# Nine pairs of seven block products in the last network's input half, two weight sums in device memory, and another order of the last products

## The chip, the cores and the metric

The kernel runs on one core of one Trainium2 chip, in float32. The metric is the device time of one execution in microseconds (us), the median of several runs.

## What is computed

One layer of a diffusion backbone on 512 latent tokens and 256 context tokens of width 1024: a gated network (input 1024 to 2 x 2816, output 2816 to 1024), a token mixer, and a second gated network for the latent tokens alone. The change is in the second network:

```python
def swiglu(h, w_in, w_out):
    gate, up = jnp.split(h @ w_in, 2, axis=-1)
    return (jax.nn.silu(gate) * up) @ w_out

x = residual_post_norm(x, swiglu(modulate(x, m, 2), ffn2_w_in[l], ffn2_w_out[l]), m[:, 8], FFN_HALF, ln_gain[2], ln_bias[2])
```

Here h is 512 x 1024, w_in is 1024 x 5632 (the left half gives the gate, the right half "up") and w_out is 2816 x 1024.

## The kernel before, in words

**Precision.** Each float32 operand is split into a high part (rounded to the type fp32r) and a low part (the rest). `product` (L2197) issues three matmuls for one product: low by high (L2199), high by low (L2200), high by high (L2201). A weight tile comes by DMA into one of two raw buffers `w_raw` (8 KB per partition, 1 MB in all); ScalarE writes its high part (`split_hi`, L957), then VectorE its low part (`split_lo`, L1448). The split tiles have two slots each in most of the kernel, three in the last network.

**Order of the work.** All weights are loaded in the order of one list, `JOBS`. Every engine walks the same list by loops written out by hand: `load` on the queue of SyncE (SP), `split_hi` on ScalarE (ACT), `split_lo` on VectorE (DVE), the products on TensorE (PE). A raw buffer is loaded again once the low part of the job that used it is written; jobs i and i+2 share a raw buffer. The splits of job i+2 are issued while PE works on job i. Each engine runs its instructions in order.

**Stages**, in time of the profile: L1, the first network on the latent tokens, to about 413 us; C, the same network on the 256 context tokens (22 input jobs, then output jobs) to about 600; the mixer (six groups of heads, g = 0 to 5) to about 946; its output projection and the norms to about 1000; L2, the second network, to the end. An input job of C is 48 matmuls of 256 columns, one of L1 or L2 has 48 matmuls of 512 columns (2 blocks of 128 output columns, gate and up, x 8 tiles of the contraction x 3).

**L2's input half** has 22 such jobs (`last_ffn` on each engine: L1054 ACT, L1707 DVE, L2366 PE). Per job ACT applies silu to the gate's PSUM bank (L1066) and DVE multiplies it with the other bank into `hid_last` (L1717). **L2's output half** is already done as seven block products in place of eight (Winograd's form): `SEVEN` is their order, each in 3 steps by 2 token tiles; sums of blocks of `hid_last` are formed on DVE (L1649), sums of blocks of w_out in device memory. PSUM banks X, Y and Z collect the products; `keep` copies an early sum out (ACT L1052), `join` combines a late one with it (DVE L1675).

**GpSimd (POOL)** issues through its own DMA queue: blocks of w_ada in L1 (L826), and in the mixer `copy_weights` (L888) and `add_weights` (L891), DMAs from device memory to device memory that copy a block of w_out and add another to it.

## Time and profile before

| | |
|---|---|
| median of 3 runs | 1336.09 us (1335.64 to 1336.14) |
| the profiled execution | 1336.66 us, span 1334.8 us |
| TensorE busy | 1307.2 us, 98% of the span; granted clock 0.994 on average |
| VectorE busy | 825.3 us, 62% |
| ScalarE busy | 546.5 us, 41% |
| DMA | 206.74 MB, mean 155 GB/s |

The span runs from the first to the last instruction. The profiled execution took 1.86 us more than its span and 0.57 us more than the median. A matmul's recorded duration overlaps with its neighbours', so the pace of matmuls is read from their starts.

### The profile page before, as it was taken

What the parts mean: (1) busy time and instruction counts of PE and PEld (TensorE: products, weight loads), DVE (VectorE), ACT (ScalarE), POOL (GpSimd) and SP (SyncE); (2) the same over time, 40 slices, a digit from 0 to 9 for tenths busy, and PEclk for the clock granted to TensorE, in tenths of its full rate; (3) what the DMA queues carried; (4) which work ended last, traced back from release to release, by engine and by line L of the source; (5) the groups of instructions that cost most, each with busy time, mean ns of one, the idle gap of its engine ahead of it and who ended that gap; (6) DMA issues with size and microseconds to landing.
All of it is one profiled execution on the core that took longest, in us unless ns stands there. A gap on an engine that the chain in (4) does not pass through costs nothing.

```text
span 1334.8 us, 17708 instructions
## 1 busy us (share of the span) xinstructions
PE 1307.2 (98%) x7134; PEld 1102.9 (83%) x7134; DVE 825.3 (62%) x1165; ACT 546.5 (41%) x740; POOL 83.0 (6%) x91
## 2 busy tenths in 40 slices
PE   8999999999999999999999999999999999999996
PEld 5778888888889999888888888887788888888885
DVE  5446688666686777565227678878763223335888
ACT  5525221222212544565325645556552222224553
POOL 1000000000000000000202221220000000000000
PEclk8999999999999999999999999999999999999998
DMA  9965545665545667553432478266435333333562
GB/s 320 275 180 175 186 164 164 185 180 172 178 158 156 177 189 190 174 174 126 138 122 64 83 200 220 54 148 150 142 95 158 95 111 95 96 95 110 190 205 102
DMA packets 217378, 206.74 MB, mean 155 GB/s; under 512 B 7322, under 2 KB 175880, under 8 KB 216592
## 3 DMA queue, kind: packets, MB, share of 16 engines
q1 hardware_dynamic: 202328, 151.39, 38.5%
q0 software_dynamic: 14272, 52.53, 13.9%
q10 hardware_dynamic: 696, 1.68, 0.4%
q8 instruction: 57, 0.93, 0.3%
q14 instruction: 25, 0.20, 0.0%
HBM read 203.46 MB, written 25.18 MB: 171 GB/s over the span
## 4 chain that ended last, share of the span: by engine, by line
PE 84%; DVE 6%; ACT 3%; issue 2%; DMA 2%; SPq 2%; DVEq 0%; ACTq 0%
PE ps L2199 27%; PE ps L2201 26%; PE ps L2200 26%; DMA w_raw<-ffn_w_in 1%; DVE w_lo L1448 1%; DMA gain_bias_b<-w_ada 1%; PE ps L2238 1%; SPq L770 1%; PE ps L2662 1%; PE ps L2647 1%; ACT w_hi L957 1%; PE ps L2251 0%; PE ps L2681 0%; SPq L766 0%; DVE xl L1570 0%
## 5 line engine op out<-in xcount | busy, mean ns | idle before, releaser
L2199 PE MATMUL ps<-h_hi,w_lo 128*128 128x512 f32 (+1 forms) x1120 | 391.5, 350 | 1.9 <-DVE w_lo L1796 1.4
L2201 PE MATMUL ps<-h_hi,w_hi 128*128 128x512 f32 (+1 forms) x1120 | 387.7, 346 | 0.0
L2200 PE MATMUL ps<-h_lo,w_hi 128*128 128x512 f32 (+1 forms) x1120 | 387.7, 346 | 0.0
L1448 DVE TENSOR_TENSOR w_lo<-w_raw,w_hi 128x2048 fp32r<-128x2048 f32 (+1 forms) x116 | 256.3, 2210 | 157.9 <-ACT w_hi L957 157.7
L957 ACT ACTIVATE w_hi<-w_raw 128x2048 fp32r<-128x2048 f32 (+1 forms) x116 | 214.2, 1848 | 274.0 <-PE ps L2201 259.9
L2199 PEld LDWEIGHTS ps<-h_hi,w_lo 128*128 128x128 f32 x1120 | 211.7, 189 | 32.2 <-issue 4.2
L2201 PEld LDWEIGHTS ps<-h_hi,w_hi 128*128 128x128 f32 x1120 | 211.7, 189 | 27.0
L2200 PEld LDWEIGHTS ps<-h_lo,w_hi 128*128 128x128 f32 x1120 | 211.8, 189 | 25.5
L2199 PE MATMUL ps<-w_hi,h_lo 128*128 128x512 f32 x298 | 117.0, 393 | 1.4 <-DVE w_lo L1448 1.4
L1460 DVE SCALAR_TENSOR_TENSOR ada_row<-ada_block,c_cols,ada_row 128x256 f32<-128x256 f32 x224 | 108.6, 485 | 8.0
L2199 PE MATMUL ps<-h_hi,half_lo 128*128 128x512 f32 (+1 forms) x272 | 101.9, 375 | 0.7 <-ACT beside_lo L1286 0.4
L1717 DVE TENSOR_TENSOR hid_last<-ps,glu 128x512 f32<-128x512 f32 x22 | 15.2, 692 | 139.4 <-ACT glu L1066 139.4
L2201 PE MATMUL ps<-w_hi,h_hi 128*128 128x512 f32 x256 | 99.7, 389 | 0.0
L2200 PE MATMUL ps<-w_lo,h_hi 128*128 128x512 f32 x256 | 99.6, 389 | 0.0
L2201 PE MATMUL ps<-h_hi,half_hi 128*128 128x512 f32 (+1 forms) x272 | 97.6, 359 | 0.0
L2200 PE MATMUL ps<-h_lo,half_hi 128*128 128x512 f32 (+1 forms) x272 | 97.5, 358 | 0.0
L1066 ACT ACTIVATE glu<-ps 128x512 f32<-128x512 f32 x22 | 13.2, 598 | 172.8 <-PE ps L2201 172.8
L2199 PE MATMUL ps<-w_hi,hid_lo_lat 128*128 128x512 f32 x176 | 69.6, 396 | 0.0
L2201 PE MATMUL ps<-w_hi,hid_hi_lat 128*128 128x512 f32 x176 | 68.6, 390 | 0.0
L2200 PE MATMUL ps<-w_lo,hid_hi_lat 128*128 128x512 f32 x176 | 68.5, 389 | 0.0
L2199 PEld LDWEIGHTS ps<-w_hi,h_lo 128*128 128x128 f32 x298 | 56.0, 188 | 13.8 <-DVE w_lo L1448 2.3
L2199 PEld LDWEIGHTS ps<-h_hi,half_lo 128*128 128x128 f32 x272 | 51.3, 189 | 10.5 <-issue 2.8
(297 smaller groups left out, 1699.5 us busy)
## 6 DMA issues: line engine op xcount, KB each, us to landing
w_raw<-ffn_w_in SPq DMA_DIRECT2D x124, 512.0 KB, 5.2
ada_block<-w_ada POOLq DMA_DIRECT2D x28, 1024.0 KB, 5.7
w_raw<-ffn_w_out SPq DMA_DIRECT2D x55, 512.0 KB, 4.3
weight_sums<-ffn_w_out POOLq DMA_DIRECT2D x6, 2816.0 KB, 21.6
half_raw<-w_mix_in SPq DMA_DIRECT2D x48, 256.0 KB, 3.4
w_raw<-weight_sums SPq DMA_DIRECT2D x20, 512.0 KB, 4.0
ada_block<-w_ada SPq DMA_DIRECT2D x6, 1024.0 KB, 9.7
weight_sums<-weight_sums POOLq DMA_DIRECT2D x2, 2816.0 KB, 17.9
```

The costliest lines, as they stand in the source:

```text
L770: sp.dma_start(dst[:, 2 * pair:2 * pair + 2, u, :], w1i[:, 2 * pair:2 * pair + 2, u * FF + j * P:u * FF + (j + 1) * P]).then_inc(s_w[pair] ...
L957: nc.scalar.activation(hi, raw, ACT.Copy).then_inc(s_hi[s], 1)
L1066: nc.scalar.activation(glu[:, j % 2, :], ps[:, hidden_bank("L2", 0, j), :], ACT.Silu).then_inc(s_silu, 1)
L1448: nc.vector.tensor_tensor(lo, raw, hi.bitcast(F32), ALU.subtract).then_inc(s_lo[s], 1)
L1460: ins = nc.vector.scalar_tensor_tensor(out=row, in0=ada_block[:, k, :], scalar=c_cols[:, k, v:v + 1], in1=row, op0=ALU.mult, op1=ALU.add)
L1717: nc.vector.tensor_tensor(hid_last[:, j, :], ps[:, hidden_bank("L2", 0, j) + 1, :], glu[:, j % 2, :], ALU.mult).then_inc(s_hf, 1)
L2199: nc.tensor.matmul(dst, s_low, m_high, start=start, stop=False, skip_group_check=shared)
L2200: nc.tensor.matmul(dst, s_high, m_low, start=False, stop=False, skip_group_check=shared)
L2201: return nc.tensor.matmul(dst, s_high, m_high, start=False, stop=stop, skip_group_check=shared)
L2238: ins = nc.tensor.matmul(ada_sums_ps[:, j, v, :], ada_row[:, v, c], ones[:, 0:2], start=True, stop=True)
L2647: ins = nc.tensor.matmul(ps[p0:p0 + pn, 5, slot * P:(slot + 1) * P], ktok[:, j, p0:p0 + pn], vtok[:, tile, v], start=j != 1, stop=j != 0, ...
L2662: ins = nc.tensor.matmul(ps[:, o_bank(g, hd), c], St[p0:p0 + pn, order(d).index(tile), :], QST[d][p0:p0 + pn, c], start=d == 0 and tile == ...
```

## The change

**Input half of L2.** The first 4 of the 22 jobs stay (`WHOLE`). The other 18 become 9 pairs. A pair computes 256 columns of the gate and 256 of up for 512 tokens as a 2 x 2 by 2 x 2 block product: two blocks of 256 tokens, two blocks of 512 of the contraction, and the column blocks gate and up. It uses seven products, P1 to P7, in place of eight. Each is 24 matmuls of 256 columns (2 column tiles x 4 contraction tiles x 3), 168 in all, in place of the 96 matmuls of 512 columns of two jobs. A pair has four weight jobs or parts: (P1, P5), (P6, P3), (P7, P2), (P4).

- Weights: part 0 loads 1 MB (a block of w_in, and the block sum of P5 from device memory), part 1 512 KB, part 2 1 MB (the block sum of P7 from device memory, and a block of w_in), part 3 nothing. The sums for P6 and P4 are formed on DVE from raw buffers (`add_inner_weights`), in place in a raw buffer. Loads of w_in have rows of 256 columns in place of 128.
- Inputs: DVE forms four block sums of h (`input_sum`, 8 instructions of 128x512) and their low parts (4 of 128x1024), ACT their high parts.
- Sums of products: ACT copies P1, P5, P6 out of PSUM (`pair_keep`), DVE joins P3, P7 and P2 with the copies (`pair_join`), ACT applies silu (`pair_silu`), DVE multiplies (`pair_hidden`) and forms `first_left_sums`. P4 is accumulated onto P7's bank, after `join` of P7.

**Two weight sums in device memory.** POOL copies eight blocks of 128x2304 of w_in (1,152 KB each) between the w_ada loads of L1, adds four such blocks in C's input half, two at the end of the mixer's group 2 and two at the end of group 5.

**Output half of L2.** P2 and P7 change places in `SEVEN`; P7's sums are copied out by ACT (`keep`) before DVE joins them, and P4 waits for the copy. The gate's turn uses PSUM bank 5. The output tiles' order in the counters follows.

The core of the diff:

```diff
-SEVEN = ("P1", "P5", "P6", "P3", "P7", "P2", "P4")
+SEVEN = ("P1", "P5", "P6", "P3", "P2", "P7", "P4")
+WHOLE = 4
+PAIRS = (22 - WHOLE) // 2
+PAIR_PARTS = (("P1", "P5"), ("P6", "P3"), ("P7", "P2"), ("P4",))
-KEPT = ("P1", "P5", "P6")
-JOINED = ("P3", "P7", "P2")
+KEPT = ("P1", "P5", "P6", "P7")
+JOINED = ("P3", "P2", "P7")
...
@@ SyncE, in load(i)
+                if key[1:2] == ("pair",):
+                    _, _, t_, part = key
+                    c0 = (WHOLE + 2 * t_) * P
+                    blocks = raw.rearrange("p (b k c) -> p b k c", k=4, c=256)
+                    if part == 0:
+                        sp.wait_ge(s_wadd, 2 * t_)
+                        sp.wait_ge(s_isum, 64)
+                        sources = (w2i[:, 0:4, c0:c0 + 256], i_sums[0][:, :, c0 - WHOLE * P:c0 - WHOLE * P + 256])
+                    elif part == 1:
+                        for k in (0, 2):
+                            sp.dma_start(blocks[:, 1, k:k + 2, :], w2i[:, 4 + k:6 + k, FF + c0:FF + c0 + 256]).then_inc(s_loaded[s], 16)
+                        return
+                    else:
+                        sp.wait_ge(s_wadd, 2 * t_ + 1)
+                        sp.wait_ge(s_isum, 128)
+                        sources = (i_sums[1][:, :, c0 - WHOLE * P:c0 - WHOLE * P + 256], w2i[:, 4:8, c0:c0 + 256])
+                    for b, src in enumerate(sources):
+                        sp.dma_start(blocks[:, b, :, :], src).then_inc(s_loaded[s], 16)
+                    return
...
@@ GpSimd
+            def add_inner(which, n):
+                pool.dma_start(split_row(inner_rows(which, n)), split_row(inner_block(which, 1, n)), accum_op=ALU.add,
+                               max_dma_last_dim=8192).then_inc(s_isum, 16)
             for m in range(ADA_FIRST, ADA_BLOCKS):
                 ada(m)
+                if m >= 14 and (m - 14) % 3 == 0:
+                    n = (m - 14) // 3
+                    copy_inner(n // 4, n % 4)
+            for n in range(4):
+                pool.wait_ge(s_hf, HID["C", 0, 4 + 5 * n] + 1)
+                pool.wait_ge(s_icopy, 128)
+                add_inner(0, n)
...
+                if g in (2, 5):
+                    for n in (0, 1) if g == 2 else (2, 3):
+                        add_inner(1, n)
...
@@ ScalarE, last_ffn
+                for t in range(PAIRS):
+                    for part in range(len(PAIR_PARTS)):
+                        pair_split_hi(JOB["L2", "pair", t, part] + 2)
+                        if part == 0:
+                            pair_keep(t, "P1")
+                            pair_keep(t, "P5")
+                        if part == 1:
+                            pair_keep(t, "P6")
+                        if part == 3:
+                            pair_silu(t, 0)
+                            pair_silu(t, 1)
...
@@ VectorE
+            def add_inner_weights(t, which):
+                first, second, third = (JOB["L2", "pair", t, part] for part in range(3))
+                blocks = [w_raw[s][:, :].rearrange("p (b n) -> p b n", n=1024) for s in (first % 2, second % 2)]
...
+                nc.vector.tensor_tensor(blocks[1][:, 0, :], a, b, ALU.add).then_inc(s_wadd, 1)
+
+            def pair_split_lo(i):
...
+                split_lo(i)
+                if JOBS[i][3] in (0, 2):
+                    add_inner_weights(JOBS[i][2], JOBS[i][3] // 2)
...
@@ VectorE, last_ffn
+                for t in range(PAIRS):
+                    for part in range(len(PAIR_PARTS)):
+                        pair_split_lo(JOB["L2", "pair", t, part] + 2)
+                        if part == 1:
+                            pair_join(t, "P3")
+                        if part == 2:
+                            pair_join(t, "P7")
+                            pair_join(t, "P2")
+                    pair_hidden(t, 0)
+                    pair_hidden(t, 1)
+                    first_left_sums(t)
...
@@ TensorE, in pair_products(t, part)
+                    if p in ("P6", "P3", "P7"):
+                        pe.wait_ge(s_kept, 3 * t + ("P6", "P3", "P7").index(p) + 1)
+                    if p == "P4":
+                        pe.wait_ge(s_joined, 3 * t + 2)
...
@@ TensorE, in seven_free(p, tile)
-                if p in ("P6", "P3", "P7"):
-                    pe.wait_ge(s_kept, 2 * ("P6", "P3", "P7").index(p) + tile + 1)
-                if p == "P4":
-                    pe.wait_ge(s_joined, 2 * JOINED.index("P7") + tile + 1)
+                if p in ("P6", "P3", "P7", "P4"):
+                    pe.wait_ge(s_kept, 3 * PAIRS + 2 * ("P6", "P3", "P7", "P4").index(p) + tile + 1)
```

How the order on two engines moves. VectorE in the input half of L2, before: per job a product into `hid_last` (line 1717) and a low part of weights (line 1448, `split_lo`).

```order
L1717 TENSOR_TENSOR hid_last<-ps,glu 128x512 [waits silu_ready,slot3_products_done]
L1448 TENSOR_TENSOR w_lo<-w_raw,w_hi 128x2048 [waits slot2_hi_ready]
L1717 TENSOR_TENSOR hid_last<-ps,glu 128x512 [waits silu_ready,slot1_products_done]
L1448 TENSOR_TENSOR w_lo<-w_raw,w_hi 128x2048 [waits slot1_hi_ready]
L1717 TENSOR_TENSOR hid_last<-ps,glu 128x512 [waits silu_ready,slot0_products_done]
L1448 TENSOR_TENSOR w_lo<-w_raw,w_hi 128x2048 [waits slot0_hi_ready]
```

A job has two instructions there, and neither waits for a load: the only waits are for ACT and PE.

The same engine in the changed kernel, one pair in the middle of the stage (line 1587 is `split_lo`, 1884 `add_inner_weights`, 1903 `pair_join`, 1909 `pair_hidden`).

```order
L1587 TENSOR_TENSOR w_lo<-w_raw,w_hi 128x2048 [waits slot1_hi_ready]
L1884 TENSOR_TENSOR w_raw<-w_raw 128x1024 [waits slot2_lo_ready,slot0_loaded]
L1587 TENSOR_TENSOR w_lo<-w_raw,w_hi 128x1024 [waits slot0_hi_ready]
L1903 TENSOR_TENSOR hid_last<-ps,hid_last 128x2x256 [waits slot2_products_done,early_sums_kept]
L1587 TENSOR_TENSOR w_lo<-w_raw,w_hi 128x2048 [waits slot2_hi_ready]
L1884 TENSOR_TENSOR w_raw<-w_raw 128x1024 [waits slot1_loaded,slot0_loaded,slot0_lo_ready]
L1903 TENSOR_TENSOR hid_last<-hid_last,ps 128x2x256 [waits first_product_of_part_or_first_tile_done,early_sums_kept]
L1903 TENSOR_TENSOR glu<-glu,ps 128x512 [waits slot1_products_done,early_sums_kept]
L1587 TENSOR_TENSOR w_lo<-w_raw,w_hi 128x2048 [waits slot1_hi_ready]
L1909 TENSOR_TENSOR hid_last<-hid_last,glu 128x2x256 [waits sums_joined,silu_ready] x2
L1916 TENSOR_TENSOR hid_last<-hid_last 128x2x256 [waits hidden_ready]
```

Per pair VectorE has four low parts, two weight sums and three joins, and the join of P7 (the second row of line 1903) stands behind the low part and the weight sum of the next pair's part 0.

GpSimd between the last blocks of w_ada and the mixer, in the changed kernel (line 888 is `ada`, 918 `copy_inner`, 921 `add_inner`):

```order
L888 DMA ada_block<-w_ada 128x8x256 [waits ada_rows_or_sums_taken] x3
L918 DMA inner_weight_sums<-ffn_w_in 128x2304
L921 DMA inner_weight_sums<-ffn_w_in 128x2x1152 [waits inner_weights_copied_for_sums,hidden_ready] x4
L937 MEMSET attT 128x512 [waits h_ready]
L937 MEMSET attT 128x512
L938 MEMSET mT 128x512
L939 MEMSET squares 128x512
```

The rows of lines 918 and 921 are new; four adding DMAs stand ahead of the mixer's memsets, each behind a wait for an input job of C.

GpSimd at the end of the mixer, in the changed kernel (line 965 is `state_queries`, 977 `add_weights`):

```order
L965 TENSOR_TENSOR qstate<-qdec,fq 128x512 [waits tile_tails_ready,readouts_done,decay_exponentials_ready,q_decayed]
L956 TENSOR_SCALAR gate<-gate 128x512 [waits silu_exp_ready]
L965 TENSOR_TENSOR qstate<-qdec,fq 128x512 [waits tile_tails_ready,readouts_done,decay_exponentials_ready,q_decayed]
L977 DMA weight_sums<-weight_sums 352x2048 [waits weight_sums_added]
L965 TENSOR_TENSOR qstate<-qdec,fq 128x512 [waits tile_tails_ready,readouts_done,decay_exponentials_ready,q_decayed]
L921 DMA inner_weight_sums<-ffn_w_in 128x2x1152 x2
L219 UNCONDITIONAL_BRANCH
```

The row of line 921 is new there: two adding DMAs stand behind the last `state_queries`.

## Rows read from the trace of the kernel before

**Rows 1.** The page: busy time and share of the span by engine.

```profile
PE 1307.2 (98%) x7134; PEld 1102.9 (83%) x7134; DVE 825.3 (62%) x1165; ACT 546.5 (41%) x740; POOL 83.0 (6%) x91
```

**Rows 2.** Order of time, ACT and DVE, 1110 to 1121: start us, duration, engine, line.

```profile
1110.02 0.60 ACT L1066 ACTIVATE glu<-ps 128x512 f32<-128x512 f32 x1 [8.48 <-PE ps L2201]
1110.51 1.91 ACT L957 ACTIVATE w_hi<-w_raw 128x2048 fp32r<-128x2048 f32 x1
1120.90 0.60 ACT L1066 ACTIVATE glu<-ps 128x512 f32<-128x512 f32 x1 [8.48 <-PE ps L2201]
...
1112.45 2.29 DVE L1448 TENSOR_TENSOR w_lo<-w_raw,w_hi 128x2048 fp32r<-128x2048 f32 x1 [0.58 <-ACT w_hi L957]
```

**Rows 3.** Order of time, ACT in C, two input jobs.

```profile
483.95 1.92 ACT L957 ACTIVATE w_hi<-w_raw 128x2048 fp32r<-128x2048 f32 x1 [0.57 <-PE ps L2201]
...
489.71 1.92 ACT L957 ACTIVATE w_hi<-w_raw 128x2048 fp32r<-128x2048 f32 x1 [0.66 <-PE ps L2201]
```

**Rows 4.** Groups by form: line, engine, shape, count | busy, mean ns | idle before.

```profile
L1649 DVE TENSOR_TENSOR hid_last<-hid_last 128x1024 f32<-128x1024 f32 x6 | 7.3, 1220 | 0.2
```

**Rows 5.** SP issue at 1103.89; issue to landing of two pieces there, and at 1213.6.

```profile
1103.89 0.99 SPq L713 DMA_DIRECT2D w_raw<-ffn_w_in  x2
...
DMA to landing us min/median/max: 4.1/4.7/5.4
...
DMA to landing us min/median/max: 3.5/4.0/4.4
```

**Rows 6.** Order of time, DVE: low part, then a join, near the end.

```profile
1307.40 2.29 DVE L1448 TENSOR_TENSOR w_lo<-w_raw,w_hi 128x2048 fp32r<-128x2048 f32 x1 [0.58 <-ACT w_hi L957]
1309.61 0.68 DVE L1675 TENSOR_TENSOR glu<-glu,ps 128x512 f32<-128x512 f32 x1
```

**Rows 7.** Who waited for whom in L1, 60 to 390 us: total, times, longest.

```profile
ACT w_hi L957 <- PE ps L2201: 192.2, 29, 10.3
```

**Rows 8.** DMA from 869 to 889 us (40 slices of 0.5 us): rate, queues, issues with landing.

```profile
GB/s 17 0 0 0 33 0 229 262 213 66 246 262 262 246 33 246 262 262 249 92 236 260 245 243 88 278 244 261 75 256 261 244 227 103 252 323 377 370 385 189
...
weight_sums<-weight_sums POOLq DMA_DIRECT2D x1, 2816.0 KB, 17.7
half_raw<-w_mix_in SPq DMA_DIRECT2D x2, 256.0 KB, 13.7
```

**Rows 9.** The page: DMA issues, KB each, median us to landing.

```profile
half_raw<-w_mix_in SPq DMA_DIRECT2D x48, 256.0 KB, 3.4
```

**Rows 10.** DMA from 880 to 884 us: packets, MB of each queue.

```profile
q0 software_dynamic: 97, 0.79, 95.2%
q1 hardware_dynamic: 97, 0.05, 6.3%
```

**Rows 11.** Issues in C: SP at 483.03, one piece, and its landing.

```profile
483.03 0.58 SPq L713 DMA_DIRECT2D w_raw<-ffn_w_in  x1
...
DMA to landing us min/median/max: 5.5/5.5/5.5
```

**Rows 12.** Order of time in C: DVE, and an ACT wait for a DMA.

```profile
482.51 0.42 DVE L1598 TENSOR_TENSOR glu<-ps,glu 128x256 f32<-128x256 f32 x1
...
461.56 1.91 ACT L957 ACTIVATE w_hi<-w_raw 128x2048 fp32r<-128x2048 f32 x1 [1.35 <-DMA w_raw<-ffn_w_in]
```

**Rows 13.** TensorE, its longest waits in the mixer, 760 to 930 us.

```profile
PE ps L2662 <- DVE state L2005: 0.9, 2, 0.7
```

**Rows 14.** Order of time at the end of the mixer: POOL, SP, ACT, DVE; the chain.

```profile
926.54 1.27 POOL L879 TENSOR_TENSOR qstate<-qdec,fq 128x512 f32<-128x512 f32 x1 [17.91 <-DVE tail_u L1975]
...
933.97 0.88 SPq L744 DMA_DIRECT2D w_raw<-w_mix_out  x2
...
940.40 1.92 ACT L957 ACTIVATE w_hi<-w_raw 128x2048 fp32r<-128x2048 f32 x1 [1.16 <-DMA w_raw<-w_mix_out]
...
943.60 2.29 DVE L1448 TENSOR_TENSOR w_lo<-w_raw,w_hi 128x2048 fp32r<-128x2048 f32 x1
...
946.06 0.38 PE ps L2199
```

More of the change, by code:

```diff
@@ L65, in ffn @@
         for part, tiles in enumerate(FFN_PARTS[tag]):
-            jobs.extend((tag, "in", part, j) for j in range(tiles))
+            jobs.extend((tag, "in", part, j) for j in range(WHOLE if tag == "L2" else tiles))
             if tag == "L2":
+                jobs.extend((tag, "pair", t, part) for t in range(PAIRS) for part in range(len(PAIR_PARTS)))
                 jobs.extend((tag, "seven", p, s) for p in SEVEN for s in range(len(SEVEN_STEPS)))
@@ L164, in out_keys @@
     if tag == "L2":
-        return [(tag, 0, half, i) for half, tiles in ((1, (0, 1)), (1, (2, 3)), (0, (0, 1)), (0, (2, 3))) for i in tiles]
+        return [(tag, 0, half, i) for half, tiles in ((1, (0, 1)), (0, (0, 1)), (1, (2, 3)), (0, (2, 3))) for i in tiles]
     tiles = TC if tag == "C" else TL
@@ L258, in build @@
             gate_b = sb("gate_b", [P, D], F32, s0)
+            with ExitStack() as s1:
+                s3_hi, s3_lo = (sb(f"third_sum_{x}", [P, 4, 256], F32R, s1) for x in ("hi", "lo"))
             xn = sb("xn", [P, D], F32, s0)
@@ L279, in build @@
                 with ExitStack() as s1:
-                    between_h = [sb(f"h_full{i}", [P, KT, P], F32, s1) for i in range(1, TL)]
                     between_xn = sb("xn_other", [P, D], F32, s1)
@@ new lines, in pair_keep @@
+            def pair_keep(t, p):
+                x = {"P1": halves(glu[:, 0, :]), "P5": hid_last[:, pair_rows(t), 256:512],
+                     "P6": hid_last[:, pair_rows(t), 0:256]}[p]
+                if p == "P5":
+                    wait_done(JOB["L2", "pair", t, 0])
+                else:
+                    act.wait_ge(s_seven, 3 * t + (1 if p == "P1" else 2))
+                if p == "P1":
+                    act.wait_ge(s_hf, pair_hid(t) - (0 if t else 1))
+                nc.scalar.activation(x, halves(ps[:, pair_bank(t, p), :]), ACT.Copy).then_inc(s_kept, 1)
@@ new lines, in pair_silu, with pair_split_hi @@
+            def pair_silu(t, late):
+                if late:
+                    wait_done(JOB["L2", "pair", t, 3])
+                    act.wait_ge(s_hf, pair_hid(t))
+                    nc.scalar.activation(glu[:, 1, :], ps[:, pair_bank(t, "P4"), :], ACT.Silu).then_inc(s_silu, 1)
+                else:
+                    act.wait_ge(s_joined, 3 * t + 3)
+                    nc.scalar.activation(glu[:, 0, :], glu[:, 0, :], ACT.Silu).then_inc(s_silu, 1)
+            def pair_split_hi(i):
+                if i >= SEVEN_FIRST:
+                    split_both_hi(i - SEVEN_FIRST)
+                else:
+                    split_hi(i)
@@ new lines, in input_sum_low @@
+            def input_sum_low(n):
+                p, slot = (("P5", 0), ("P6", 1), ("P7", 1), ("P3", 0))[n]
+                dve.wait_ge(s_lefthi, n + 1)
+                hi, lo = pair_left(p)
+                nc.vector.scalar_tensor_tensor(out=lo, in0=h_sums[slot][:, :, :], scalar=left_sign(p), in1=hi.bitcast(F32),
+                                               op0=ALU.mult, op1=ALU.subtract).then_inc(s_leftlo, 1)
+            def add_inner_weights(t, which):
+                first, second, third = (JOB["L2", "pair", t, part] for part in range(3))
+                blocks = [w_raw[s][:, :].rearrange("p (b n) -> p b n", n=1024) for s in (first % 2, second % 2)]
+                if which == 0:
+                    if t:
+                        last = JOB["L2", "pair", t - 1, 3]
+                        dve.wait_ge(s_lo[slot_of(last)], USES[last] + 1)
+                    for i in (first, second):
+                        dve.wait_ge(s_loaded[i % 2], 32 * RAW_LOADS[i])
+                    a, b = blocks[0][:, 1, :], blocks[1][:, 1, :]
+                else:
+                    dve.wait_ge(s_loaded[third % 2], 32 * RAW_LOADS[third])
+                    dve.wait_ge(s_lo[slot_of(second)], USES[second] + 1)
+                    a, b = blocks[1][:, 0, :], blocks[0][:, 1, :]
+                nc.vector.tensor_tensor(blocks[1][:, 0, :], a, b, ALU.add).then_inc(s_wadd, 1)
@@ new lines, in pair_split_lo, with pair_join @@
+            def pair_split_lo(i):
+                if i >= SEVEN_FIRST:
+                    split_both_lo(i - SEVEN_FIRST)
+                    return
+                split_lo(i)
+                if JOBS[i][3] in (0, 2):
+                    add_inner_weights(JOBS[i][2], JOBS[i][3] // 2)
+            def pair_join(t, p):
+                rows, bank = pair_rows(t), halves(ps[:, pair_bank(t, p), :])
+                dve.wait_ge(s_kept, 3 * t + {"P3": 3, "P7": 2, "P2": 1}[p])
+                y = {"P3": hid_last[:, rows, 0:256], "P7": hid_last[:, rows, 256:512], "P2": halves(glu[:, 0, :])}[p]
+                if p == "P7":
+                    dve.wait_ge(s_seven, 3 * t + 3)
+                else:
+                    wait_done(JOB["L2", "pair", t, 1 if p == "P3" else 2])
+                a, b = (bank, y) if p == "P3" else (y, bank)
+                nc.vector.tensor_tensor(y, a, b, ALU.add if p == "P2" else ALU.subtract).then_inc(s_joined, 1)
```

215 lines of the change are left out of this document (158 added, 57 removed).

## The prediction

> **What bounds the kernel now.** First the page: TensorE is busy for 1307.2 us of the span of 1334.8 [rows 1]. So in nearly every stage what counts is TensorE's own work, and anything that makes it wait adds to the end. In the input half of the last network (L2) the other engines have room: ScalarE waits 8.48 us of each job for TensorE [rows 2]. The question is what is left of that room, and of the DMA's, once the work is cut up.
>
> **The matmuls.** Two silus of L2 are 10.88 us apart [rows 2], for 48 matmuls of 512 columns: 0.227 us each. In C two high parts that wait for TensorE are 5.76 us apart [rows 3], for 48 matmuls of 256 columns: 0.120 us each. A pair had 96 of the first kind, 21.76 us; it gets 168 of the second, 20.16 us. The columns fall by an eighth, the time by only 1.60 us, since the shorter matmul costs more per column. Nine pairs: 14.4 us, if nothing waits.
>
> **The pair's chains.** Something does. Take times from the start of a pair: parts 0, 1, 2 are 5.76 us each, part 3 (P4) should start at 17.28. Prices: start of a high part to start of its low part 1.94 us, low part 2.29 [rows 2]; a sum of 128x1024 1.22 [rows 4].
>
> *Chain of loads.* Part 0 and part 2 use the same raw buffer. Part 2's load waits until part 0's low part and the weight sum after it are done; then high part, low part, a second sum; only then may the next pair's part 0 be loaded. One turn is two loads, two high parts, two low parts, two sums, and no product of TensorE is in it. A load of 1 MB took 5.9 us from its first issue when its rows were 512 bytes (issue 1103.89, second piece some 0.5 later, landed 5.4 after that), and about 4.8 for 2 KB rows (4.4 after the second issue) [rows 5]. The new rows are 1 KB, in neither row. I take 5.2, nearer the first because w_in keeps its stride; the ends are 4.8 and 5.9. One turn is then 2 x (5.2 + 1.94 + 2.29 + 1.22 + some 0.1 of handing over) = 21.5 us, against 20.16 of products. The wait shows at P4, which needs the join of P7: 0.68 us [rows 6], queued on VectorE behind that low part and sum. The first pair's loads come early. For it the shorter chain counts, from the end of part 1 (the slot comes free): 1.94 + 2.29 + 1.22 + 0.68 and some 0.3 of handing over is 6.4 us, where P7 and P2 cover 5.76: 20.8 us. Sum: 20.8 + 8 x 21.5 = 192.8 us, where the 18 jobs took 195.8: **-3.0 us**. With the ends of the load: -9 us (at 4.8 the shorter chain nearly takes over; it alone would give -8.6) and +8 us (22.9 a pair).
>
> The rest of the pair fits: VectorE's 14.7 us (four low parts 8.1, two sums 2.4, three joins 2.0, two products 1.4, a left sum 0.7) and ScalarE's 9 or so lie under 20 us, and the copies of P1, P5 and P6 each have a product of 2.88 us between their end and the next use of the bank. If the load chain went, VectorE's order would be late next.
>
> **The added transfers.** Copies in L1, eight of 1,152 KB: they delay loads by some 4 us each, but ScalarE waits 192.2 us in 29 times for TensorE there (6.6 us each) [rows 7]. Cost 0; without that cover up to 1 us each.
>
> The adding DMAs are what I weigh most. In the mixer, one of 2,816 KB takes 17.7 us to land and moves nothing in its first 2 us: 180 KB per us at most. While it ran, loads of 256 KB took 13.7 us [rows 8], against 3.4 on the page [rows 9]. The packets say why: in four us each queue moved 97, but the adding queue's held 8 KB and the load's 512 bytes [rows 10]. One packet each in turn, so the load gets what its packets are worth. The new ones have rows of 4.6 KB: an added DMA of 1,152 KB blocks the engines for about 6.4 us, and a load of 512-byte rows gets a tenth of its usual rate. The Trainium skill (DMA: Bandwidth & Descriptors, Queues, rings and completion order) says an engine takes turns between rows at packets of typically 9 to 17 descriptors; small rows would then be grouped and lose far less. The row of 13.7 us speaks against that here; what it would give is a rival below.
>
> In C the load is issued at 483.03 and lands 5.5 us later, 488.5 [rows 11]; ScalarE's high part starts at 489.71 [rows 3], 1.2 us of slack. Its low part ends 4.2 us after, TensorE needs it 5.76 after: 1.4 us more. The add is issued at the product into `glu`, done at 482.93 [rows 12], and moves data from 484.7 to 491.1, over three quarters of that load. The load lands 5.8 us late; less 2.6 of slack, TensorE waits 3.2 us. The phase is the same for the second and third add. The first falls where a load was late already (ScalarE waited 1.35 us for it [rows 12]): at least as much, say 3.2. The fourth meets a load of 2 KB rows, which gets four times the share: 1.5. Sum **+11.1 us**; bounds 2 (the load gets through) and 16.
>
> Group 2: the same starving in the mixer left TensorE's longest waits at 0.9 us in two times [rows 13]: 0, at most 2.
>
> Group 5: POOL is through with its last instruction at 927.8, so 2,304 KB move from about 929.5 to 942.3. The load of the output projection is issued at 933.97, its high part at 940.40 waited 1.16 us for it, its low part ends at 945.89, and TensorE starts on it at 946.06 [rows 14]: no slack. That load has rows of 2 KB beside packets of 4.6 KB, so three tenths of the bandwidth: some 60% of it is through by 942.3, and it lands about 3.3 us late. The norms behind are a chain and shift with it: **+3.3 us**, bounds 0 and 6.
>
> **Head and end, together.** The sums of h (12 VectorE instructions, 10.4 us, and the loads) fall where VectorE idled before the first products; 0, at most +1. At the end P7's copy is issued behind a high part that ended at 1307.4, as P2's join was behind a low part, 1309.61 [rows 6]; P4 starts after that: 0, within 0.5. The reordered tiles save two instructions of 0.1.
>
> **Sum.** -3.0 + 11.1 + 3.3 = +11.4, with 0.5 for small waits **+12 us**. The profiled execution took 1336.66 us; it would take 1348.7, and the median, 0.57 below it, 1348.
>
> **The rivals.**
> A. *Packets are grouped* (the rule above): both queues share alike. A load in C then lands some 3 us late, about the slack: C +3, group 5 +1.5, pairs -3: 1338 us. For it: some loads in C came 1.35 us late without harm. Against: 13.7 us for 256 KB.
> B. *Faster: the transfers hide, and the load chain runs at 2 KB speed.* Decides if 1 MB lands within 4.9 us and a load loses under 2.6 us per add: pairs -8, C and group 5 +2: 1330 us. For it: the mixer ran beside such transfers with no wait of TensorE. Against: in C each job's load is needed every 5.76 us, in the mixer a load waited 13.7 and was still early.
> C. *Slower still: the load chain at 512-byte speed*, as reads from two tensors share the turn: pairs +8, the rest as forecast: 1359 us.
> D. *The change doesn't give what it says*: fewer columns but the same time, if matmuls of 256 columns ran slower beside the loads of weights than in C. The pace in C speaks against it [rows 3]; it would give 1350 to 1365.
>
> **How the numbers follow.** Forecast 0.53, A 0.13, B 0.20, C 0.09, D 0.05. The forecast's own range, from its bounds, is 1340 to 1355. The whole range, 1330 to 1358, takes in A, D, about half of B and of C, and leaves out their far halves and the ends. About 0.2% (2.7 us) is what a measurement of this kernel can tell from none. Faster: B and a sliver of A and the forecast's low end, 0.22; within 0.2%: most of A, 0.10; slower 0.68.
>
> **What would show it.** In the changed profile: matmuls of 256 columns 0.120 us apart in L2; a wait of some 1.3 us at P4 per pair, released by VectorE's join; ScalarE waiting for a DMA at each pair's parts 0 and 2; four waits of some 3 us in C behind late loads; a late high part at 940. I am wrong if TensorE is busy throughout C, or if pairs are 20.8 us or less apart.

## The result, and the profile after

The changed kernel takes **1360.7 us** (median of 4 runs: 1356.55, 1356.90, 1364.50 and 1365.33, two clusters), the kernel before 1335.87 in the same comparison: ratio 1.0192, interval 1.0170 to 1.0213. It is slower by 24.8 us, where 12 were forecast, and the time lies outside the range. The direction was right, the size was not.

The profiled execution took 1356.55 us, with a span of 1354.7. It is the shortest of the four, so it shows 19.9 us of the loss; what is known of the rest stands with the last experiment.

The page of the changed kernel, its row of busy time (answers to [rows 1]) and its DMA row of the copies and adds:

```profile
PE 1299.8 (96%) x7782; PEld 1125.4 (83%) x7782; DVE 901.7 (67%) x1235; ACT 593.6 (44%) x791; POOL 96.3 (7%) x107
...
inner_weight_sums<-ffn_w_in POOLq DMA_DIRECT2D x16, 1152.0 KB, 9.5
```

TensorE has 7.4 us less work and is idle for 27 us more. The waits of TensorE in three stretches of the changed kernel (who waited for whom: total us, times, longest), C, the end of the mixer, and the pairs:

```profile
PE ps L2424 <- DVE glu L1737: 10.0, 4, 5.8
PE ps L2476 <- DVE xn L1639: 2.3, 1, 2.3
```

```profile
PE ps L2424 <- DVE h_lo L2268: 4.9, 1, 4.9
```

```profile
PE ps L2424 <- DVE hid_last L1903: 11.8, 8, 2.3
```

What stands behind the first and second of these is on ScalarE: high parts that wait for a load. In order of time, ScalarE of the changed kernel (start, duration, engine; in brackets the idle time ahead and what ended it):

```profile
465.38 1.91 ACT L1048 ACTIVATE w_hi<-w_raw 128x2048 fp32r<-128x2048 f32 x1 [6.94 <-DMA w_raw<-ffn_w_in]
...
959.62 1.91 ACT L1048 ACTIVATE w_hi<-w_raw 128x2048 fp32r<-128x2048 f32 x1 [7.85 <-DMA w_raw<-w_mix_out]
961.43 0.61 ACT L1453 ACTIVATE h_hi<-mT 128x512 fp32r<-128x512 f32 x1
```

The same high parts started at 461.56 [rows 12] and 940.40 [rows 14] before. The third row is a second victim: the last high part of the mixer's output stands behind the waiting one in ScalarE's order, and TensorE waits 4.9 us for its low part (`h_lo`).

The waits are not all. TensorE in stretches of 2 us behind these two waits in the changed kernel (us, busy time and count, granted clock, DMA share, GB/s; count of matmuls that started):

```profile
466.00:468.00 2.00, 0.00 (x0) 0.67 0.46 110
468.00:470.00 2.00, 0.00 (x0) 0.50 0.01 3
470.00:472.00 2.00, 1.84 (x8) 0.50 0.54 137
472.00:474.00 2.00, 2.00 (x13) 0.63 1.11 317
474.00:476.00 2.00, 2.00 (x19) 1.00 0.36 88
...
961.00:963.00 2.00, 0.18 (x1) 0.65 1.17 332
963.00:965.00 2.00, 1.47 (x3) 0.50 0.84 332
965.00:967.00 2.00, 1.85 (x4) 0.50 0.25 75
967.00:969.00 2.00, 2.00 (x7) 0.64 1.10 313
969.00:971.00 2.00, 2.00 (x10) 1.00 0.65 156
```

After each wait the granted clock was 0.50 (1.2 GHz in place of 2.4): matmuls of 256 columns start 8 in 2 us and then 19. In C the lowered stretch began while TensorE was still idle and cost about 1.7 us, half of the 3.3 that TensorE worked in it; at 961 about 2.5, half of 4.9. Before, the granted clock was 1.00 in both stages.

The ledger, from the starts of the same high parts in both traces:

| stretch | start before | start after | shift | change | forecast |
|---|---|---|---|---|---|
| last of C before the first add | 454.69 | 452.91 | -1.8 | -1.8 (start of the program) | 0 |
| end of C | 564.71 | 577.25 | +12.5 | +14.3 | +11.1 |
| behind group 5 | 971.65 | 992.38 | +20.7 | +8.2 | +3.3 |
| last job before the pairs | 1022.93 | 1044.61 | +21.7 | +1.0 (sums of h) | 0 to +1 |
| end of the span | 1334.8 | 1354.7 | +19.9 | -1.8 | -3.0 |

L1 and the rest of the mixer moved nothing, as forecast. Of the 14.3 us in C the first add took 7.1 (the shift against before goes from -1.8 to +5.3 by the second add) and each of the other three 2.4, where the prediction had 3.2, 3.2, 3.2 and 1.5.

### The profile page after: what moved, and what is told of

Read it like the earlier page. It is cut to its first block, busy times and chain, and to the rows that moved or that the text cites. A ratio compares the mean times of both kernels' runs of the same rounds, so it can differ in the third digit from the quotient of the medians.

```text
span 1354.7 us, 19277 instructions
## 1 busy us (share of the span) xinstructions
PE 1299.8 (96%) x7782; PEld 1125.4 (83%) x7782; DVE 901.7 (67%) x1235; ACT 593.6 (44%) x791; POOL 96.3 (7%) x107
## 4 chain that ended last, share of the span: by engine, by line
PE 71%; DMA 9%; DVE 8%; ACT 5%; issue 5%; SPq 2%; DVEq 0%; ACTq 0%
PE ps L2424 22%; PE ps L2426 22%; PE ps L2425 22%; DMA w_raw<-ffn_w_in 5%; ACT w_hi L1048 3%; DVE w_lo L1587 2%; DMA w_raw<-inner_weight_sums 1%; DVE w_raw L1884 1%; DMA w_raw<-w_mix_out 1%; DMA gain_bias_b<-w_ada 1%; PE ps L2463 1%; SPq L830 1%; DMA w_raw<-ffn_w_out 1%; PE ps L2914 1%; PE ps L2899 1%
## 5 line engine op out<-in xcount | busy, mean ns | idle before, releaser
L1587 DVE TENSOR_TENSOR w_lo<-w_raw,w_hi 128x2048 fp32r<-128x2048 f32 (+3 forms) x134 | 287.9, 2149 | 207.2 <-ACT w_hi L1048 207.0
L2424 PE MATMUL ps<-h_hi,w_lo 128*128 128x256 f32 (+1 forms) x1264 | 403.1, 319 | 22.4 <-DVE hid_last L1903 11.8
L1048 ACT ACTIVATE w_hi<-w_raw 128x2048 fp32r<-128x2048 f32 (+3 forms) x134 | 241.0, 1799 | 371.5 <-PE ps L2426 259.9
L2425 PE MATMUL ps<-h_lo,w_hi 128*128 128x256 f32 (+1 forms) x1264 | 398.4, 315 | 0.0
L2426 PE MATMUL ps<-h_hi,w_hi 128*128 128x256 f32 (+1 forms) x1264 | 398.4, 315 | 0.0
L2424 PEld LDWEIGHTS ps<-h_hi,w_lo 128*128 128x128 f32 x1264 | 241.2, 191 | 43.7 <-issue 20.3
L2426 PEld LDWEIGHTS ps<-h_hi,w_hi 128*128 128x128 f32 x1264 | 241.1, 191 | 15.6
L2425 PEld LDWEIGHTS ps<-h_lo,w_hi 128*128 128x128 f32 x1264 | 241.2, 191 | 14.3
L2426 PEld LDWEIGHTS ps<-h_hi,half_hi 128*128 128x128 f32 x272 | 51.3, 189 | 7.9
L2425 PEld LDWEIGHTS ps<-h_lo,half_hi 128*128 128x128 f32 x272 | 51.4, 189 | 7.6 <-issue 1.0
## 6 DMA issues: line engine op xcount, KB each, us to landing
weight_sums<-ffn_w_out POOLq DMA_DIRECT2D x6, 2816.0 KB, 21.6
```

The source lines that it names most:

```text
L1048: nc.scalar.activation(hi, raw, ACT.Copy).then_inc(s_hi[s], 1)
L1587: nc.vector.tensor_tensor(lo, raw, hi.bitcast(F32), ALU.subtract).then_inc(s_lo[s], 1)
L2424: nc.tensor.matmul(dst, s_low, m_high, start=start, stop=False, skip_group_check=shared)
L2425: nc.tensor.matmul(dst, s_high, m_low, start=False, stop=False, skip_group_check=shared)
L2426: return nc.tensor.matmul(dst, s_high, m_high, start=False, stop=stop, skip_group_check=shared)
```

## Experiments

Each was compared with the kernel before on the same chip, whose median lay between 1334.6 and 1335.0 us.

**Transfers and pairs apart.** `transfers_only` is the kernel before with the copies and adds alone:

```diff
             for m in range(ADA_FIRST, ADA_BLOCKS):
                 ada(m)
+                if m >= 14 and (m - 14) % 3 == 0:
+                    n = (m - 14) // 3
+                    copy_inner(n // 4, n % 4)
+            for n in range(4):
+                pool.wait_ge(s_hf, HID["C", 0, 4 + 5 * n] + 1)
+                pool.wait_ge(s_icopy, 128)
+                add_inner(0, n)
...
+                if g in (2, 5):
+                    for n in (0, 1) if g == 2 else (2, 3):
+                        add_inner(1, n)
```

> The kernel before with the eight copies and eight adding DMAs put in where the changed kernel has them; nothing reads the sums, and L2 is as before. Theory 1 (the adding DMAs starve the loads beside them, in C and behind group 5; that is all of the loss): the profile after showed about 12 us more in C and 7 us more at 940 to 960, so +19 us, 1355 us. Theory 2 (a good part of the loss sits in the pairs or in the end): +8 us or less, under 1344 us. If the second cluster of times (1365) shows here too, it belongs to the transfers.

Measured: 1358.42 us, ratio 1.0173 (1.0157 to 1.0188), +23.4 us. All four runs lie in 1356.3 to 1359.1: the cluster at 1365 does not show here.

`pairs_only` is the changed kernel with these lines taken out, and

```diff
-                        sp.wait_ge(s_isum, 64)
-                        sources = (w2i[:, 0:4, c0:c0 + 256], i_sums[0][:, :, c0 - WHOLE * P:c0 - WHOLE * P + 256])
+                        sources = (w2i[:, 0:4, c0:c0 + 256], w2i[:, 4:8, c0:c0 + 256])
...
-                        sp.wait_ge(s_isum, 128)
-                        sources = (i_sums[1][:, :, c0 - WHOLE * P:c0 - WHOLE * P + 256], w2i[:, 4:8, c0:c0 + 256])
+                        sources = (w2i[:, 0:4, c0:c0 + 256], w2i[:, 4:8, c0:c0 + 256])
```

The loads keep their sizes and the length of their rows, but P5 and P7 use other weights, so this kernel leaves out the layer's right result; so do `early_block` and `p7_first` below, which are built on it.

> The changed kernel without the copies and adds; the pairs load other blocks of w_in in place of the two sums, so P5 and P7 use wrong weights (sizes and rows of the loads are the same). Theory 1: L2's change alone is worth what the load chain leaves, -1 to -3 us: 1333 to 1335 us, with P3's joins 21.7 us apart. Theory 2 (the pairs lose time): 1340 us or more. One cluster of times by theory 1.

Measured: 1335.93 us (10 runs, 1332.54 to 1340.38), ratio 1.0006 (0.9996 to 1.0016). The two add up: 23.4 and 0.9 are 24.3 of the 24.8 us. Nearly the whole loss is the transfers', and an eighth fewer columns bring nothing. Why, one pair of the changed kernel shows on ScalarE and SyncE, in order of time:

```profile
1136.59 0.60 ACT L1163 ACTIVATE hid_last<-ps 128x512 f32<-128x512 f32 x1 [1.65 <-PE ps L2426]
...
1139.47 0.60 ACT L1163 ACTIVATE hid_last<-ps 128x512 f32<-128x512 f32 x1 [0.47 <-PE ps L2426]
1143.28 1.92 ACT L1048 ACTIVATE w_hi<-w_raw 128x2048 fp32r<-128x2048 f32 x1 [3.21 <-DMA w_raw<-inner_weight_sums]
1148.69 1.91 ACT L1048 ACTIVATE w_hi<-w_raw 128x2048 fp32r<-128x2048 f32 x1 [3.49 <-DVE w_raw L1884]
...
1154.22 1.92 ACT L1048 ACTIVATE w_hi<-w_raw 128x2048 fp32r<-128x2048 f32 x1 [1.08 <-DMA w_raw<-ffn_w_in]
```

```profile
1127.01 0.37 SPq L772 DMA_DIRECT2D w_raw<-inner_weight_sums  x1
...
1148.72 0.37 SPq L772 DMA_DIRECT2D w_raw<-inner_weight_sums  x1
```

Two products of 24 matmuls are 2.88 us apart (1136.59, 1139.47): 0.120 us each, as in C. The load of part 2 is issued at 1127.01 and again at 1148.72, 21.71 us later. In each turn the high parts (line 1048) wait for loads (3.21, 1.08) or weight sums (3.49) and never for a product; only the copies out of PSUM (line 1163) wait for TensorE. That is the forecast's chain of loads, forecast at 21.5.

**Packets.** `adds_small` cuts the adding DMAs finer:

```diff
-                               max_dma_last_dim=8192).then_inc(s_isum, 16)
+                               max_dma_last_dim=512).then_inc(s_isum, 16)
```

> The changed kernel with the adding DMAs cut into packets of 512 bytes in place of 4.6 KB. Theory 1 (one packet of each queue in turn): the loads get half the engines' packets in place of a tenth, C loses 3 to 5 us and group 5 some 2 us: 1340 to 1345 us. Rival (the bytes moved beside the load count, however they are cut; small packets take longer in sum): 1356 us or more, waits of 2 to 6 us in C as now.

Measured: 1362.68 us, ratio 1.0214 (1.0197 to 1.0231): the theory fell and the rival held. Its DMA view from 461 to 464.5 us (a load of C beside an add), and that of the changed kernel from 458 to 462:

```profile
q0 software_dynamic: 692, 0.35, 79.1%
q1 hardware_dynamic: 688, 0.35, 50.4%
```

```profile
q0 software_dynamic: 172, 0.79, 98.1%
q1 hardware_dynamic: 139, 0.07, 8.6%
```

With packets of one size the queues do share packet by packet, 692 to 688, and alike in bytes. But the first add now lands after 17.6 us in place of 12.4. The load issued ahead of it at 451 us landed 9.1 us after its issue in place of 14.0, the next one 13.0 in place of 11.2, and TensorE waited 0.9 and 4.3 us there in place of 5.8. At the later adds it waited 2.7 to 3.3 us each in place of 1.6 to 2.3, and C lost 20.1 us in place of 14.3. The longer neighbour took away more than the fairer share gave. The Trainium skill (DMA: Bandwidth & Descriptors, Queues, rings and completion order) has an engine drain a packet of typically 9 to 17 descriptors before it turns to the next queue. Read as the prediction read it (small rows are grouped and keep their share of the bytes), it is not borne out: in the changed kernel the packets alternate nearly one for one, and the load got 0.07 MB of 0.86.

**Adds where there is room.** `adds_in_l1` adds each block in L1, two w_ada blocks behind its copy:

```diff
-                if m >= 14 and (m - 14) % 3 == 0:
-                    n = (m - 14) // 3
-                    copy_inner(n // 4, n % 4)
+                if 10 <= m <= 31 and (m - 10) % 3 == 0:
+                    n = (m - 10) // 3
+                    copy_inner(n // 4, n % 4)
+                if m >= 12 and (m - 12) % 3 == 0:
+                    n = (m - 12) // 3
+                    pool.wait_ge(s_icopy, 16 * n + 16)
+                    add_inner(n // 4, n % 4)
```

> The changed kernel with all eight adding DMAs in L1, each some two w_ada blocks behind its copy; C and the mixer have none. ScalarE has 6.6 us of slack a job in L1 and an add blocks the engines for about 6.4 us. Theory 1: the loads there come late but are waited for little, 0 to 4 us in all: 1333 to 1338 us. Rival (the adds starve the loads by more than the slack wherever they are): 1 to 2 us each, 1342 to 1350 us.

Measured: 1340.82 us, ratio 1.0039 (1.0025 to 1.0052), between the two expectations. Seven of the eight adds moved no high part. The third, issued at 181.61 behind the w_ada block of 180.74, made that block late: TensorE's longest wait in L1,

```profile
PE ps L2460 <- DVE ada_row L1596: 2.4, 1, 2.4
```

and from one high part (184.71) to the next (202.18) the shift against before went from -1.9 to +3.8 us. The granted clock was 0.50 for 6.8 us from 195.4 on. The slack of 6.6 us a job was there; the victim was another transfer.

**The load chain.** `early_block` issues a pair's first block without waiting for the weight sum (in `pairs_only`; in `best1` the same beside the real sources):

```diff
-                        sp.wait_ge(s_wadd, 2 * t_)
...
-                        sp.wait_ge(s_wadd, 2 * t_ + 1)
...
                     for b, src in enumerate(sources):
+                        if b:
+                            sp.wait_ge(s_wadd, 2 * t_ + part // 2)
                         sp.dma_start(blocks[:, b, :, :], src).then_inc(s_loaded[s], 16)
```

> The pairs without transfers (pairs_only), and of each 1 MB load the first block is issued as soon as the low part that used the buffer is written; only the second block waits for the weight sum. Theory (the chain of loads, low parts and sums through one raw buffer sets the pair, 21.5 us and more, and its waits of some 2 us at P4 are followed by stretches at granted clock 0.5): the turn falls by 0.8 to 1.2 us for each of two loads, to 19.5 to 20 us, the shorter chain of the first pair (20.8) takes over, and the lowered stretches go: 20.8 us a pair, 7 us less than pairs_only, 1329 us, 1326 if the waits vanish wholly. Rival (the load's end is set by bandwidth, not by its start): joins still 21.5 apart, 1334 us or more.

Measured: 1331.20 us, ratio 0.9970 (0.9960 to 0.9980), 4.7 us less than `pairs_only`. `p7_first` changes VectorE's order alone:

```diff
+                        if part == 2:
+                            pair_join(t, "P7")
                         pair_split_lo(JOB["L2", "pair", t, part] + 2)
                         if part == 1:
                             pair_join(t, "P3")
                         if part == 2:
-                            pair_join(t, "P7")
                             pair_join(t, "P2")
```

> The pairs without transfers (pairs_only), VectorE's join of P7 issued ahead of the low part and weight sum of the next pair's first job. By the chain theory P4 waits for nothing but P7, and the turn of loads stays 21.5 us: the wait moves to the start of the next pair once its slack of 2 to 3 us is used up. That gives 2 to 3 us once, and fewer lowered stretches: 1330 to 1333 us. Rival (VectorE's order is the bound, not the load chain): pairs of 20.2 to 20.5 us, 1324 us.

Measured: 1328.50 us, ratio 0.9951 (0.9932 to 0.9970): 7.4 us less than `pairs_only`, more than the theory expected and less than the rival. `best1` has both edits, the adds of `adds_in_l1` with the harmful one moved from block 18 to block 20, and the right sums:

> All of it with right results: copies and adds in L1, the one add moved that delayed a w_ada block at 181 us (it cost 2.4 us of wait and 3.4 of lowered clock in adds_in_l1), the first block of each pair's load ahead of the weight sum, and the join of P7 first. Theory: the transfers cost 0 to 1 us, pairs run at 20.2 to 20.8 us: 1321 to 1328 us. If adds in L1 cost wherever they are: 1330 us or more.

Measured: 1330.28 us (10 runs, 1323.66 to 1334.19), ratio 0.9966 (0.9952 to 0.9979). It beats both kernels, by less than expected. Its profile shows the shortest of the ten, 6.6 us under the median; there the adds in L1 moved nothing. But the median is 1.8 us above that of `p7_first`, which has no transfers, and no run shows what the other nine lost. The joins of P3, first and last of nine, in `pairs_only`, `early_block`, `p7_first` and `best1` (one engine's lines: duration min/median/max, first and last start):

```profile
L1891 DVE TENSOR_TENSOR hid_last<-ps,hid_last x9: 691/692/693, 1032.4 to 1208.5; 128x512 f32<-128x512 f32 x9
```

```profile
L1891 DVE TENSOR_TENSOR hid_last<-ps,hid_last x9: 691/692/692, 1031.2 to 1202.4; 128x512 f32<-128x512 f32 x9
```

```profile
L1891 DVE TENSOR_TENSOR hid_last<-ps,hid_last x9: 691/692/692, 1032.5 to 1202.3; 128x512 f32<-128x512 f32 x9
```

```profile
L1900 DVE TENSOR_TENSOR hid_last<-ps,hid_last x9: 691/692/692, 1031.9 to 1197.4; 128x512 f32<-128x512 f32 x9
```

Eight pairs take 176.1, 171.2, 169.8 and 165.5 us: 22.0, 21.4, 21.2 and 20.7 each. Part of that is the clock: among these eight pairs `pairs_only` has two stretches of 3.4 us at 0.50, `early_block` one, the other two none. With up to 1.7 us off for each, the pairs take 21.6, 21.2, 21.2 and 20.7 us. Each edit alone still shortens them and both together more, so loads and VectorE's order were both part of the wait at P4. In `p7_first` TensorE no longer waits for a join but for ScalarE's copies,

```profile
PE ps L2413 <- ACT glu L1151: 6.2, 8, 1.3
```

and these stand behind a high part that waits for a load: what is left there is the load chain, at 21.2 us. Products alone are 20.16.

**Smaller adds.** `halves_g2`:

```diff
-            for n in range(4):
-                pool.wait_ge(s_hf, HID["C", 0, 4 + 5 * n] + 1)
+            for n in range(8):
+                pool.wait_ge(s_hf, HID["C", 0, 4 + 2 * n] + 1)
                 pool.wait_ge(s_icopy, 128)
-                add_inner(0, n)
+                add_half(0, n // 2, n % 2)
...
-                if g in (2, 5):
-                    for n in (0, 1) if g == 2 else (2, 3):
+                if g == 2:
+                    for n in range(4):
                         add_inner(1, n)
```

`add_half` adds one half of a block, 576 KB; SyncE's waits for the sums follow.

> The changed kernel with C's four adding DMAs of 1,152 KB cut into eight of 576 KB, one behind every second job, and group 5's two moved to group 2. Theory (an add holds back the load beside it for its own length, 6.2 us, now 3.1; a load in C has 2.6 us of slack, and only a wait of several us is followed by a lowered clock): 0.5 us or less for each in C and no lowered stretch, group 2 costs 0 to 2: 1336 to 1341 us. Rival (the cost goes by the bytes added, 4.6 MB in C): C still loses 8 to 12 us, 1345 us or more.

Measured: 1356.39 us, ratio 1.0152 (1.0130 to 1.0175); the sum was wrong, the part for C half right. From the first add to the end of C the high parts shift by 4.0 us in place of 14.3, but a wait of 2.6 us behind the first half was followed by a lowered stretch, which the theory had ruled out. But four adds in one group cost more than the two of the changed kernel, which cost nothing there: the mixer's waits, 600 to 940 us, and the stretch's granted clock:

```profile
PE ps L2904 <- ACT ktok L1408: 6.4, 1, 6.4
...
600.00:940.00 340.00, 330.82 (x1936) 0.98 0.57 143
```

**What a wait costs.** The last four runs ask for the price of a wait. `first_add_later`:

```diff
-                pool.wait_ge(s_hf, HID["C", 0, 4 + 5 * n] + 1)
+                pool.wait_ge(s_hf, HID["C", 0, (7, 10, 14, 19)[n]] + 1)
```

> The changed kernel with C's first two adding DMAs behind jobs 7 and 10 in place of 4 and 9. In the profile after, the add behind job 4 meets a load that was late already: TensorE waits 5.8 us there and then runs 6.8 us at granted clock 0.5, 3.4 us more. Theory (the price of a late load has a second part, the lowered clock, which only waits of several us bring): C loses 7 to 9 us in place of 14, and no lowered stretch stands in C: 6 us less than the changed kernel, 1350 to 1355 us. Rival (each add costs the same 3.5 us wherever it is): 1356 to 1361 us as before.

Measured: 1353.93 us (1350.71 to 1363.16), ratio 1.0155 (1.0118 to 1.0192), 6.8 us less than the changed kernel's 1360.7, near the 6 expected, though the intervals of the two overlap. TensorE's waits from 413 to 600 us:

```profile
PE ps L2424 <- DVE glu L1737: 5.7, 3, 2.5
```

The long wait is gone, but only part of the theory held. C lost 10.0 us where 7 to 9 were expected (the shift of the high parts goes from -1.8 to +8.3), and a stretch of 3.4 us at 0.50 stays in C, behind a wait of 2.4 us, where none was expected. It isn't so that only waits of several us are followed by one.

`g5_one` and `g5_two` are the kernel before with the copies, and one or both adds of group 5:

```diff
+                if g == 5:
+                    pool.wait_ge(s_icopy, 128)
+                    for n in (2,):
+                        add_inner(1, n)
```

> The kernel before with the copies in L1 and one single adding DMA, at the end of group 5. The add blocks from about 930 to 936, the output projection's load is issued at 934. Theory: the load comes 2 us late at most, TensorE waits 0 to 2 us, no lowered stretch: 1335 to 1337 us. Rival (the wait is for the queue as a whole, half of what two adds cost): +4 us, 1339 us.

> As g5_one with both adding DMAs of group 5. Theory: the changed kernel's cost there, 4.9 us of wait and 3.4 us of lowered clock: +8 us, 1343 us. Rival (the forecast's price, the late load alone, with no part of the clock): +3 to +5 us, 1338 to 1340 us.

Measured: 1335.85 us, ratio 1.0009 (1.0000 to 1.0019), for one add, and 1344.13 us, ratio 1.0069 (1.0054 to 1.0084), for two. The first add costs 1.3 us, the second 8.3. Of `g5_two`, TensorE's wait, and its stretches of 2 us behind it:

```profile
PE ps L2226 <- DVE h_lo L2070: 4.9, 1, 4.9
```

```profile
948.00:950.00 2.00, 1.19 (x3) 0.69 1.06 381
950.00:952.00 2.00, 1.32 (x4) 0.50 0.42 168
952.00:954.00 2.00, 2.00 (x6) 0.50 0.78 229
...
956.00:958.00 2.00, 2.00 (x10) 1.00 0.02 3
```

and the same 20 us of `g5_one`, without a lowered clock:

```profile
940.00:960.00 20.00, 19.29 (x90) 1.00 0.47 140
```

`after_again` is the changed kernel, to see where its times differ from run to run.

> The changed kernel itself again. Its four times lie at 1356.6, 1356.9, 1364.5 and 1365.3. Theory: the spread is the number of lowered stretches behind waits of some 2 us (at P4 and in C), each 1.7 or 3.4 us, so the times fill the range from 1354 to 1366 rather than two clusters, and a longer execution shows more stretches at 0.5. Rival (a second state of the transfers): two clusters 8 us apart again, with the same stretches.

Measured: 1356.85, 1359.65, 1363.10 and 1366.30 us (median 1361.38, ratio 1.0200, 1.0172 to 1.0228), which fill the gap between the two clusters. The profiled execution has a span of 1361.3 us, 6.6 more than the first. Its waits are no longer, in C and in the pairs:

```profile
PE ps L2424 <- DVE glu L1737: 9.3, 3, 5.4
...
PE ps L2424 <- DVE hid_last L1903: 11.1, 8, 2.9
```

Its clock is lower. Stages of the changed kernel, first the earlier execution, then this one (from 413, 1000 and 1045 us on):

```profile
413.00:600.00 187.00, 174.38 (x1271) 0.98 0.71 190
...
1000.00:1045.00 45.00, 42.31 (x308) 1.00 0.25 76
1045.00:1250.00 205.00, 193.16 (x1549) 1.00 0.43 135
```

```profile
413.00:600.00 187.00, 175.03 (x1260) 0.96 0.71 189
...
1000.00:1045.00 45.00, 43.13 (x314) 0.96 0.28 82
1045.00:1250.00 205.00, 193.79 (x1546) 0.98 0.41 129
```

The record of the clock holds five more stretches of 3.4 us at 0.50 (from 508.9, 573.7, 1007.2, 1068.7 and 1113.0 us on): at most 5 x 1.7 = 8.5 us, where the spans differ by 6.6. So between these two executions the waits are nearly equal and the difference is the clock's. Which wait is followed by such a stretch is not the same in two executions of one program; by what rule was not tried.

That doesn't hold for the whole spread. Each execution has its mean granted clock on record, and of the first four, 1356.90 us had 0.988 and 1364.50 us had 0.989: 7.6 us apart without more time at the low clock. In `pairs_only` the longest of ten, 1340.38 us, had one of the two highest clocks, 0.994. `transfers_only` spread over 2.8 us in four runs, `pairs_only` over 7.8 in ten. Something else spreads these times too, and no kept trace shows it.

## Why the prediction was wrong in size

- **Matmuls, 0.120 us for 256 columns**: right (2.88 us for 24). Rival D fell.
- **The pair's load chain**, 21.5 us a turn: right in kind, 21.7 measured; the nine joins of P3 are 21.9 us apart on average, and from the last job before the pairs to the end 1.8 us were gained in place of 3.0. The chain was not the only thing late: "if the load chain went, VectorE's order would be late next" was too generous, since with the loads as they were `p7_first` gained 0.4 us a pair besides what the clock gave back. The first pair's 20.8 was not reached: its successor's join came 22.4 us after its own.
- **The adds starve the loads**: right, and the largest term, as forecast. C was forecast at 11.1 us of waits behind loads; TensorE waited 10.0 us there. Single waits were off: the first, "at least as much, say 3.2", was 5.8, since that load was late already and had no slack to take off; behind the second add 1.6, behind the third 2.2 and 0.4, behind the fourth 2.3, for VectorE's `xn`.
- **The step that failed** is in these sentences: "less 2.6 of slack, TensorE waits 3.2 us", and for group 5 "lands about 3.3 us late. The norms behind are a chain and shift with it: +3.3 us". A wait was priced at its own length. The runs show a second part: behind the waits of 5.8 and 4.9 us TensorE worked at a granted clock of 0.50, for 1.7 and 2.5 us more in the profiled execution. In C the waits (10.0 and 2.3) and this part (1.7) make 14.0 of the 14.3 us. [rows 1] come from an execution whose clock stood at 1.00 throughout these stages, so nothing in them gave this a price; it should have stood in the range as an unknown with a cost above nothing.
- **Group 5 was mis-sized besides.** The share was as forecast, three tenths: from 950 to 954 us the loads of the changed kernel moved 0.29 MB of 0.94, packet for packet with the adds. But they had got nothing before that:

```profile
q0 software_dynamic: 151, 0.62, 103.7%
...
q0 software_dynamic: 141, 0.65, 82.6%
q1 hardware_dynamic: 142, 0.29, 22.8%
```

  (The first row is the whole view from 947 to 950 us, the others that from 950 to 954.) The load is issued at 946.47 and its first packet moves at 950.0, 3.5 us later; before it was 1.0 us, and 1.6 beside the one add of `g5_one`. Why it starts so late behind two adds is open. The adds moved data until 956.0, 9.5 us after that issue where 8.3 were forecast. From its issue to its high part it was 13.2 us in place of 6.4, so 6.7 late in place of 3.3. And the high part of the mixer's last output is queued behind it on ScalarE, so that TensorE waited 4.9 us where 3.3 were forecast. With the clock (2.5) and 0.7 more for low parts, that is about the 8.2.
- **The other 5 us** between +19.9 and the +24.8 of the medians: the profiled execution was the shortest of four, and the changed kernel's times spread over 10 us. In the second profile of it five more lowered stretches account for the 6.6 us more; for the rest of the spread the cause is open. A forecast against one execution's span carries over to a median only for a kernel without such a spread; the four times of the kernel before were 1335.3 to 1336.1.
- L1's copies, the two adds in group 2, the sums of h (+1.0) and the end: right.
- Rivals A (packets are grouped) and B (the transfers hide) fell; C's load chain at 512-byte speed (22.9 us a pair) was not seen either.

## What to carry to other kernels

A wait of TensorE costs its length and, behind it, sometimes a stretch at half the clock (1.7 to 3.4 us more here); give it a place in the range, and take into account that it helps to make the time spread. Here an adding DMA with rows of 4.6 KB delayed the loads of small rows beside it by nearly the time in which it moved data (the first one moved data for some 6 us, and the high part behind the load came 5.6 us late): put such a transfer where every load has that much slack (in L1, in `best1`, which is 0.34% faster than the kernel before), or cut it into pieces (4.0 us in C in place of 14.3), not into smaller packets. Where the engine that computes gets faster, look for the cycle of buffers that does not contain it: here loads, splits and sums through two raw buffers took 21.7 us however few columns TensorE had.

## What the runs showed of the hardware

- Short waits lowered the clock too, but not each time. In `pairs_only` TensorE waited 2.1 us at P4, and its stretches of 2 us were then:

```profile
1145.00:1147.00 2.00, 0.25 (x3) 1.00 0.00 0
1147.00:1149.00 2.00, 1.69 (x11) 0.77 0.53 157
1149.00:1151.00 2.00, 2.00 (x11) 0.50 1.04 360
```

  In the same trace another wait of 2.1 us (at 1038) was followed by none, nor were the eight at P4 in the first profile of the changed kernel. The wait of 1.9 us in the norms ahead of L2 stands in thirteen of the fourteen kept traces, that of the kernel before among them; in four (`pairs_only`, `p7_first`, `g5_two`, `after_again`) a stretch of 3.4 us at 0.50 followed. All ten waits of 4.2 us or more behind the first 60 us of these traces were followed by one. The Trainium skill (TensorE: Matmul & The Clock Gate, HAM oscillation) describes a kernel whose waits for DMA lower the clock again and again. This trace agrees in that a wait is followed by the low clock, here also with waits that come from a join on VectorE, but only after three of its waits.
- The queue of adding DMAs and that of the loads took packets nearly one for one whatever their sizes: 692 and 688 with 512 bytes on both, 172 and 139 with 4.6 KB beside 512 bytes, 141 and 142 beside 2 KB. So the size of a packet set its queue's share of the bytes.
- The price of transfers is far from linear: one add at the end of group 5 cost 1.3 us, two 9.5; two in group 2 cost nothing, four 9.5 us (the shift of the high parts went from 2.4 us at the end of C to 11.9 in group 4), of which 6.4 are the wait above and about 3 the low clock behind it.
